# Two of the four weight sums of the seven-product pairs formed by accumulating DMAs

## The reference, cut to what matters

```python
h = rmsnorm(x, g_norm)
a_u, a_v, a_z, b_q, b_k, b_v, b_gd, b_z, c_q, c_z, gl = split(h @ w_in)   # 1024 x 1024 blocks of w_in
...
out_c = cross_attn(c_q, mk, mv) * silu(c_z)            # 4 heads of 256, 256 memory tokens
gates = sigmoid(gl + b_gate)                           # three blocks of 1024: GA, GB, GC
merged = sum over branches of gates[i] * (outs[i] @ w_branch[i])
x = x + merged @ w_out
```

## Time and profile before

| | |
|---|---|
| median of 3 runs | 845.06 us (844.96 to 846.5) |
| profiled execution, its own time | 844.88 us |
| its span | 843.0 us |
| PE busy | 832.5 us, 99% of the span |
| DVE busy | 484.6 us, 57% |
| ACT busy | 401.1 us, 48% |
| POOL busy | 67.6 us, 8% |
| HBM traffic | 149 GB/s over the span |

### The profile page before, as it was taken

One profiled execution on the slowest core, in us unless ns is written; L12 is line 12 of the kernel. 1 busy time (PEld: TensorE's weight loads), 2 busy tenths in 40 slices (PEclk: granted clock), 3 DMA queues, 4 the chain that ended last, 5 costly groups with the idle time before them and its releaser, 6 DMA issues.

```text
span 843.0 us, 16407 instructions
## 1 busy us (share of the span) xinstructions
PE 832.5 (99%) x6827; PEld 810.5 (96%) x6827; DVE 484.6 (57%) x828; ACT 401.1 (48%) x691; POOL 67.6 (8%) x122
## 2 busy tenths in 40 slices
PE   8999999999999999999999999999999999999997
PEld 8999999999999999999999999999888999999995
DVE  6526533645545465423335799455678988755534
ACT  7534446356766643332232243332238777733424
POOL 1001000000000213100011211000110000000000
PEclk9999999999999999999999999999999999999999
DMA  9325843331232659623546963424563432362302
GB/s 305 98 80 164 263 150 101 100 102 52 69 133 75 214 180 325 238 95 103 175 158 223 349 211 101 141 101 150 205 245 101 150 113 88 100 227 82 120 1 102
DMA packets 87206, 126.22 MB, mean 150 GB/s; under 512 B 3114, under 2 KB 73816, under 8 KB 87136
## 3 DMA queue, kind: packets, MB, share of 16 engines
q1 hardware_dynamic: 73328, 76.58, 28.2%
q0 software_dynamic: 13712, 48.57, 16.2%
q10 hardware_dynamic: 96, 0.06, 0.0%
HBM read 112.98 MB, written 12.22 MB: 149 GB/s over the span
## 4 chain that ended last, share of the span: by engine, by line
PE 97%; DVE 1%; DMA 1%; ACT 1%; issue 0%; SPq 0%; ACTq 0%; DVEq 0%
PE mm L1315 55%; PE mm L1352 9%; PE mm L1272 6%; PE mm L1287 5%; PE mm L1261 3%; PE mm L1605 2%; PE mm L1687 2%; PE p L1246 1%; PE p L1248 1%; PE p L1247 1%; PE mm L1626 1%; PE mm L1625 1%; PE mm L1624 1%; PE p L1564 1%; PE p L1534 1%; DMA raw<-in_w_in_dram 1%
## 5 line engine op out<-in xcount | busy, mean ns | idle before, releaser
L1821 DVE TENSOR_TENSOR w_lo<-raw,w_hi 128x1024 fp32r<-128x1024 f32 x114 | 138.7, 1220 | 84.2 <-ACT w_hi L631 82.9
L1315 PE MATMUL mm<-h_lo,w_hi 128*128 128x260 f32 (+1 forms) x832 | 170.1, 286 | 0.0
L1315 PE MATMUL mm<-h_hi,w_hi 128*128 128x260 f32 (+1 forms) x832 | 167.4, 283 | 0.0
L1315 PE MATMUL mm<-h_hi,w_lo 128*128 128x260 f32 (+1 forms) x832 | 167.1, 282 | 0.0
L1315 PEld LDWEIGHTS mm<-h_lo,w_hi 128*128 128x128 f32 x832 | 128.0, 188 | 2.5 <-issue 2.4
L1315 PEld LDWEIGHTS mm<-h_hi,w_lo 128*128 128x128 f32 x832 | 128.1, 188 | 0.0
L1315 PEld LDWEIGHTS mm<-h_hi,w_hi 128*128 128x128 f32 x832 | 128.1, 188 | 0.0
L631 ACT ACTIVATE w_hi<-raw 128x1024 fp32r<-128x1024 f32 x114 | 118.9, 1052 | 11.9 <-DMA raw<-in_w_mem_kv_dram 6.1
L1315 PE MATMUL mm<-x_lo,w_hi 128*128 128x260 f32 (+1 forms) x448 | 96.2, 284 | 0.0
L1315 PE MATMUL mm<-x_hi,w_hi 128*128 128x260 f32 (+1 forms) x448 | 95.3, 283 | 0.0
L1315 PE MATMUL mm<-x_hi,w_lo 128*128 128x260 f32 (+1 forms) x448 | 95.2, 282 | 0.0
(11 more groups left out here) (446 smaller groups left out, 1766.5 us busy)
## 6 DMA issues: line engine op xcount, KB each, us to landing
raw<-in_w_in_dram SPq DMA_DIRECT2D x43, 1024.0 KB, 5.2
raw<-in_w_branch_dram SPq DMA_DIRECT2D x12, 1024.0 KB, 5.1
raw<-in_w_mem_kv_dram SPq DMA_DIRECT2D x8, 1024.0 KB, 5.9
gate<-in_cache_mem_k_dram POOLq DMA_DIRECT2D x16, 512.0 KB, 6.4
tok<-in_cache_mem_v_dram POOLq DMA_DIRECT2D x14, 512.0 KB, 5.3
tok<-in_state_gla_dram POOLq DMA_DIRECT2D x8, 512.0 KB, 7.2
out_dram<-tok POOLq DMA_DIRECT2D x8, 512.0 KB, 7.6
work<-scr_q POOLq DMA_DIRECT2D x8, 512.0 KB, 5.0
```

The costliest lines, as they stand in the source:

```text
L1315: ins = MM(mm[:, j % 2, a, 0:c1 - c0], wp[:, j, k, :], xp[:, k, c0:c1], start=(k == 0 and wp is w_hi and xp is xl), stop=(k == KT - 1 and ...
L1821: V.tensor_tensor(w_lo[:, j], raw[:, j // 2, :, (j % 2) * P:(j % 2 + 1) * P], f32(w_hi[:, j]), ALU.subtract).then_inc(split_done, 1)
```

## The change

POOL gets the sums S1 and S3. For S1 it issues a DMA that reads A22 from DRAM and adds it onto A21 in `raw`; for S3 one that reads A21 from DRAM and adds it onto A11, once A11 has been split. Each is 256 KB, 512 rows of 512 bytes. DVE keeps S2 and S4, and waits for both DMAs of a pair (`sums_loaded`) ahead of S2. The order of units becomes A11, A12, S2, then S3 with S1; `pair_sums` moves on DVE from part 0 to part 1, behind A12. The head loads and the pair sums alternate in POOL's queue.

```diff
-            for h in range(CH):
+            def odd_tile(q, r):
+                cols = slice((q % 4) * 2 * P + P, (q % 4) * 2 * P + 2 * P)
+                return source[FAST[q // 4]][r * KH * P:(r + 1) * KH * P, cols].rearrange("(k p) c -> p k c", p=P)
+            def pair_sums(q):
+                if q >= 1:
+                    pool.wait_ge(sem("sums_loaded"), 32 * q)
+                pool.wait_ge(w_loaded[q % 2], 16 * (2 * BLK[FAST[0]] + q // 2 + 1))
+                pool.dma_start(raw_part(q, "S1"), odd_tile(q, 1), accum_op=ALU.add).then_inc(sem("sums_loaded"), 16)
+                pool.wait_ge(sem("unit_lo"), 4 * q + 1)
+                pool.dma_start(raw_part(q, "S3"), odd_tile(q, 0), accum_op=ALU.add).then_inc(sem("sums_loaded"), 16)
+            def load_head(h):
                 if h >= 1:
                     pool.wait_ge(sem("ap_lo"), 3 * h)
                 ...
+            load_head(0)
+            for q in range(PAIRS):
+                pair_sums(q)
+                if q % 2 == 0 and q // 2 + 1 < CH:
+                    load_head(q // 2 + 1)
@@ ACT, pair_ahead
                 elif part == 1:
+                    unit_hi("A12", q)
+                else:
                     unit_hi("S2", q)
-                else:
                     sums_hi(q)
-                    unit_hi("A12", q)
@@ DVE, pair_sums, last_sum
             def pair_sums(q):
-                dve.wait_ge(sem("unit_lo"), 4 * q + 1)
-                link(V.tensor_tensor(raw_part(q, "S3"), raw_part(q, "A11"), raw_part(q, "A21"), ALU.add))
-                V.tensor_tensor(raw_part(q, "S1"), raw_part(q, "A21"), raw_part(q, "A22"), ALU.add)
+                dve.wait_ge(sem("sums_loaded"), 32 * (q + 1))
                 V.tensor_tensor(s2_sum, raw_part(q, "S3"), raw_part(q, "A22"), ALU.add).then_inc(sem("sums"), 1)
...
-                dve.wait_ge(sem("unit_lo"), 4 * q + 4)
+                dve.wait_ge(sem("unit_lo"), 4 * q + 3)
@@ DVE, pair_ahead
                 elif part == 0:
                     unit_lo("A11", q)
+                elif part == 1:
+                    unit_lo("A12", q)
                     pair_sums(q)
-                elif part == 1:
+                else:
                     unit_lo("S2", q)
-                else:
+                    last_sum(q)
                     sums_lo(q)
-                    unit_lo("A12", q)
-                    last_sum(q)
@@ DVE, pairs, q == 0
                     last_lo(0)
-                    pair_sums(1)
```

More of the change, by code:

```diff
@@ L1326, in product @@
                 else:
-                    pe.wait_ge(sem("unit_lo"), 4 * q + {"A11": 1, "S2": 2, "S3": 3, "S1": 3, "A12": 4}[unit])
+                    pe.wait_ge(sem("unit_lo"), 4 * q + {"A11": 1, "A12": 2, "S2": 3, "S3": 4, "S1": 4}[unit])
                 if q == 0 and name in ("P4", "P5", "P6", "P7"):
@@ L1851, in unit_lo @@
             def unit_lo(unit, q):
-                dve.wait_ge(sem("unit_hi"), 4 * q + {"A11": 1, "S2": 2, "A12": 4}[unit])
+                dve.wait_ge(sem("unit_hi"), 4 * q + {"A11": 1, "A12": 2, "S2": 3}[unit])
                 src = s2_sum if unit == "S2" else raw_part(q, unit)
@@ L1858, in sums_lo @@
             def sums_lo(q):
-                dve.wait_ge(sem("unit_hi"), 4 * q + 3)
+                dve.wait_ge(sem("unit_hi"), 4 * q + 4)
                 if slot("S3", q) < 7:
```

## The result

| | before | after |
|---|---|---|
| median | 845.57 us, 4 runs (844.96 to 846.5) | 869.78 us, 4 runs (868.49 to 871.47) |
| ratio | | 1.0287, 95% interval 1.0264 to 1.0309 |
| profiled execution | 844.88 us | 870.48 us |
| its span | 843.0 us | 868.6 us |

The change makes the kernel 24 us slower. The forecast was 857, with 868 as the end of its range: the sign was right, and the 12 us forecast are half of what came.

A forecast was written before the change was run, and what follows sets the result against it. PE was taken as the bound, busy 832.5 of 843.0 us, so only its waits count: 5.0 + 0 + 7.2 = 12.2 us over the 845.06 median gives 857. Own range 852 to 866; 8 in 10, 850 to 868.

The forecast's parts named there:

- So the change can only move the time through PE's waits: Whole kernel: PE's products and their order stay, so only waits removed or added on PE count.
- PE's busy time and clock unchanged: Sign expected in the changed kernel's trace: PE as busy as before and at the same clock.
- DVE's work, the gain at the transposes: About 10 us less work on DVE; the first transpose's 1.3 us wait (L1461, pair 0) shrinks by 0.9 us.
- Pair 0: Both sums land at 633.1 and hold up DVE: 5.0 us lost at P5 and, smaller, at the scores; range 4.3 to 8.4.
- Pair 1: S2's addition behind the division takes back 0.8 of the 0.9 us gained; put at 0, bounds -0.9 and +3.
- Pairs 3, 5 and 7: Late S2 delays pT_lo: 1.6 us each with a free DMA, 2.4 each with a 4.7 us landing, 7.2 for three.
- Pairs 2, 4 and 6: Some 7 us between A11's low part and S2's addition leave room for the landing: 0 lost.
- The sum of the waits: 5.0 for pair 0, 0 for pair 1 and 7.2 for pairs 3, 5 and 7: 12.2 us; ends 8.2 and 29.4.
- the accumulating DMA is slow: Rival, chance 0.10: landings take 8 us and more; pairs 3, 5, 7 lose 6 each, the first two pairs 11: 874.
- DVE's new place is all: Landing within 3.95 us of issue, so pairs 3, 5 and 7 lose 4.8 instead of 7.2: 855; 0.2 of the forecast.

The follow-up runs named there:

- e3: The change, but pair 0's S3 and S1 are formed on DVE at their place before, with no DMA for that pair: 862.81 us.
- e4: The change, but POOL issues pair 0's two accumulating DMAs ahead of the first head's loads instead of behind them: 863.84 us.
- e1: The change's order of units and late S2, but S3 and S1 stay on DVE in part 0 and no DMA adds: 853.4 us.
- e5: The kernel before, with accumulating DMAs and the new order in pairs 2, 4 and 6 alone: 846.77 us, ratio 1.001.
- e2: The change, but its 16 DMAs copy and don't add, so the additions of S1 and S3 are left out: 862.56 us.
- e7: The kernel before, no added DMA; DVE repeats the instruction of pT_lo three more times for heads 1 to 3: 860.95 us.
- e6: The kernel before, no added DMA; DVE repeats the instruction of pT_lo two more times for heads 1 to 3: 854.7 us.
- e8: The kernel before and its order, but in pairs 1 to 7 S1 alone comes by early DMA, S2 = A11 + S1, S3 = S2 - A22: 844.06 us.

## Why the prediction was right or wrong

For the waits the mechanism was right: both places, their order and their releasers. The step that failed is the one on which the sum stands, **"So the change can only move the time through PE's waits"**, which comes back at the end of the list of what would show it as "PE's busy time and clock unchanged". It put PE's work behind a wait at its old price without a reason. It cost 9.1 of the 25.6 us; with them the forecast would have been some 866. The size of the waits was off as well, by 3.2 us, two thirds of it in pairs 3, 5 and 7.

Over the pairs the trace of before couldn't warn of it, since its longest wait there was 1.3 us. At its very end it could. PE's last matmul, and windows of the kernel before, read as those above:

```profile
836.58 0.40 PE L1626 MATMUL mm<-x_hi,h_hi 128*128 128x512 f32 x1
```

```profile
837.00:839.00 2.00, 0.00 (x0) 0.00 (x0) 0.86 (x2) 1.02 (x3) 0.00 (x0) 1.00 0.00 0
839.00:841.00 2.00, 0.00 (x0) 0.00 (x0) 0.75 (x1) 0.72 (x1) 0.00 (x0) 0.69 0.17 61
841.00:843.00 2.00, 0.00 (x0) 0.00 (x0) 0.00 (x0) 0.00 (x0) 0.00 (x0) 0.50 0.53 201
```

The matmul ends at 837.0 and the granted clock goes from 1.00 to 0.50 at 839.8, after 2.8 us without work. The range for pairs 3, 5 and 7 held waits as long as that.

Point by point:

- **DVE's work, the gain at the transposes.** 10 us less busy, right (484.6 to 474.4). The gain was put at 0.9 and is 1.0.
- **Pair 0.** 5.0 said, 5.91 measured as one wait at P5; the smaller second one at the scores did not come, as DVE had caught up. The term was mis-sized by the landing: 634.35, not 633.1, on the clock of before. It lies within its range (4.3 to 8.4). e3 and e4 show that this place is POOL's queue and DVE's standing before L1901 together: the sums on DVE remove the wait, and an earlier issue removes 3.3 of it.
- **Pair 1.** Net 0 said; 1.18 lost and 1.0 gained. e1, without a DMA, has 1.17 there: it is DVE's order.
- **Pairs 3, 5 and 7.** 2.4 each said, 2.74, 3.21 and 3.37 measured, 9.3 in place of 7.2. The floor of 1.6 from DVE's order is confirmed by e1 (1.69, 1.67, 1.68), and the landing of 4.7 us for pair 3 too (4.6; in pairs 5 and 7 it grew to 4.8 and 5.3). The step that was too small is the landing, put at 4.7 from the end of A11's low part: the sum left out the 0.3 us from there to the issue.
- **Pairs 2, 4 and 6.** 0 said; no wait stands there in the trace of the change, but e5 has one of 1.2, behind a landing of 6.7 us in pair 6, where the "some 7 us" of room were 6.3.
- **The sum of the waits.** 12.2 said, 15.4 measured, within its bounds of 8.2 to 29.4. With them alone the time would have been 860.5, within the range; the clock took it over the end, 868.

The Trainium skill (DMA: Bandwidth & Descriptors, the section on the anatomy of a DMA on the software path) gives, by its formula, an estimate of 2.6 us for such a DMA. The trace does not agree: none of the sixteen landed in under 4.6 us, and none of the plain ones of e2 in under 3.2.

How the 24 us divide, by kernels: DVE's order alone 8.0 (e1), a DMA in place of DVE's additions a further 9.2 (e2 less e1), the adding with its smaller packets 7.2 (the change less e2). Each of the last two has clock in it, which is why neither is the sum of its waits; and since the number of falls differs between executions, the border between the two is rough.

Of the rivals, *the accumulating DMA is slow* gave the nearest time, 874, by luck, for its reason did not hold: in the change landings of 8 us and more occurred only in the crowd ahead of pair 0. *DVE's new place is all* (855) has the 4.8 us that e1 shows in pairs 3, 5 and 7 (5.0), but also 5.0 for pair 0, which e1 doesn't have; that e1 took 853.4 is other waits, in pair 1 and for the low parts, and no support for it.

The Trainium skill (TensorE: Matmul & The Clock Gate, the section on HAM oscillation) tells that gaps in which PE waits for data, when they are long enough, send its clock back to half, and that this is paid anew at each gap. The rows of e7 agree: 3.3 us of wait, then 0.50, three times. It speaks against this change, and I had not weighed it; the prediction should have had a rival with this price.

Open stays why the clock held behind 3.19 us in e4, and behind 2.05 to 2.20 in e6, and fell behind 1.98 in e2. The rows show all of them, and no run here separates what differs between them.

## What to carry to other kernels

Where PE is the bound, price a new wait of PE as the wait plus what the clock may take behind it: for waits of 2 us and more here that was another 1.5 to 3.0 us wherever it fell, and waits up to 1.8 us cost themselves alone. A sum that moves from an engine to a DMA is only as early as the DMA's issue, 0.3 us behind its releaser, plus its landing, 4.3 us at best here and 5.9 to 6.7 for S3 in the pairs with room (e5); so put the consumer that far behind, or leave it where it is. And when one step takes a later place in an in-order engine, price that move first, with the transfer at nothing: it alone was 8 of the 24 us here.

## What the hardware showed unexpectedly

- The granted clock of PE is 0.50 after waits of 1.98, 2.27, 2.57, 2.74 and 2.94 to 5.91 us, falls in the wait or up to about 1 us after PE's restart, and is back 3 to 6 us after the restart. It is 1.00 throughout after 0.7 to 1.79, in one execution after 2.05, 2.05 and 2.20, and once after 3.19.
- Added up over windows of 1 us, a fall costs PE 1.5 to 1.7 us of work in eleven of the sixteen cases of the change, e2, e3, e4 and e7, and 2.6 to 3.0 in the other five. The five are those where the clock fell about 0.8 us or more ahead of PE's restart: behind 5.91 and 3.37 in the change, 4.89 in e2, 3.38 in e3 and the last 3.30 in e7. A longer wait need not be one of them: 3.31 in e7 cost 1.6 and 1.7.
- An accumulating DMA of 512 rows of 512 bytes shows 1.27 us of issue on POOL, a plain one 0.75; where two stand together, the second starts 0.8 us behind the first (624.70 and 625.52). It landed in 4.6 us at the least in the change (4.5 in e3 and e5, 4.3 in e8), the plain ones in 3.2 (S1) and 3.8 (S3). A landing in the crowded stretch ahead of pair 0 took 10.2, and 9.2 plain: there most of the time is the queue and not the adding.
